# S5 outputs in one burst of matmuls over four groups of 32 output rows, S5 inputs as plain float32, two groups at a time

## The reference

```python
lam_bar = jnp.exp(lam * dt)
b_bar = ((lam_bar - 1.0) / lam)[..., None] * b_c
ug = u.astype(f32).reshape(bsz, seq, S5_GROUPS, S5_GROUP)
bu = jnp.einsum('blgh,gph->blgp', ug.astype(jnp.complex64), b_bar)
state = linear_scan(jnp.broadcast_to(lam_bar, bu.shape), bu)
y = jnp.einsum('blgp,ghp->blgh', state, c_c).real + d.astype(f32) * ug
y = jax.nn.gelu(y.reshape(bsz, seq, BRANCH))
y = y * jax.nn.sigmoid(y @ w_glu.astype(f32) + b_glu.astype(f32))
```

## Time and profile before

| | |
|---|---|
| runs shown | 2974.36 us median (2973.3 to 2975.58) |
| the profiled execution's own time | 2973.05 us |
| span of the profile | 2971.0 us |
| PE busy | 2894.8 us, 97% of the span |
| PE weight loads busy | 2454.7 us, 83% |
| DVE busy | 2010.5 us, 68% |
| ACT busy | 1582.0 us, 53% |
| POOL busy | 751.4 us, 25% |
| mean DMA rate | 176 GB/s |
| mean granted TensorE clock | 0.993 |

### The profile page before, as it was taken

One profiled execution on the slowest core, in us unless ns is written; L12 is line 12 of the kernel. 1 busy time (PEld: TensorE's weight loads), 2 busy tenths in 40 slices (PEclk: granted clock), 3 DMA queues, 4 the chain that ended last, 5 costly groups with the idle time before them and its releaser, 6 DMA issues.

```text
span 2971.0 us, 56245 instructions
## 1 busy us (share of the span) xinstructions
PE 2894.8 (97%) x16280; PEld 2454.7 (83%) x16280; DVE 2010.5 (68%) x3316; ACT 1582.0 (53%) x2828; POOL 751.4 (25%) x813
## 2 busy tenths in 40 slices
PE   6999999999999999999989999999999999999997
PEld 5878888888888888888877788888888888888886
DVE  7788888755555667555568888887555555665555
ACT  5555554565555655444455554546555655644443
POOL 3145445401000123111123544543000011221110
PEclk9999999999999999999999999999999999999998
DMA  6655555655555556777745555555555555577775
GB/s 225 213 174 159 162 159 154 170 170 168 159 158 164 165 156 195 209 214 209 206 142 174 167 162 159 159 162 171 171 157 164 160 168 154 158 213 209 215 209 176
DMA packets 276414, 522.69 MB, mean 176 GB/s; under 512 B 30912, under 2 KB 33872, under 8 KB 275280
## 3 DMA queue, kind: packets, MB, share of 16 engines
q1 hardware_dynamic: 257360, 477.13, 54.8%
q10 hardware_dynamic: 18944, 44.18, 4.5%
HBM read 508.60 MB, written 16.78 MB: 177 GB/s over the span
## 4 chain that ended last, share of the span: by engine, by line
PE 46%; DVE 2%; issue 2%; ACT 1%; DVEq 0%; POOL 0%; ACTq 0%; POOLq 0%
PE ps L294 26%; PE ps L293 13%; PE ps L443 1%; PE ps L337 1%; DVE w L975 1%; PE ps L456 0%; PE ps L452 0%; PE ps L296 0%; PE ps L325 0%; PE ps L338 0%; DVE zb L1523 0%; PE ps L326 0%; PE ps L327 0%; PE ps L304 0%; PE ps L313 0%
## 5 line engine op out<-in xcount | busy, mean ns | idle before, releaser
L294 PE MATMUL ps<-hb,w 128*128 128x512 f32 x5824 | 2059.1, 396 | 7.3 <-POOL hb L1553 6.1
L975 DVE TENSOR_TENSOR w<-raw,w 128x512 fp32r<-128x512 f32 x1760 | 1290.2, 738 | 859.5 <-ACT w L590 845.1
L590 ACT ACTIVATE w<-raw 128x512 fp32r<-128x512 f32 x1760 | 1098.2, 629 | 1138.6 <-PE ps L294 1135.9
L293 PE MATMUL ps<-hb,w 128*128 128x256 f32 x5690 | 1632.4, 287 | 13.2 <-DVE w L975 11.8
L294 PEld LDWEIGHTS ps<-hb,w 128*128 128x128 f32 x5824 | 1092.9, 188 | 250.5 <-issue 6.7
L293 PEld LDWEIGHTS ps<-hb,w 128*128 128x128 f32 x5690 | 1076.0, 189 | 70.8 <-issue 29.3
L294 PE MATMUL ps<-gl,w 128*128 128x512 f32 x640 | 226.6, 395 | 0.0
L1576 POOL TENSOR_TENSOR xx<-g,tab 128x512 f32<-128x512 f32 x64 | 121.0, 1891 | 269.6 <-DVE g L1038 269.1
L1703 POOL TENSOR_TENSOR nf<-zb 128x256 f32 (+1 forms) x60 | 51.9, 864 | 537.1 <-DVE zb L1491 531.6
L294 PE MATMUL ps<-w,hb 128*128 128x512 f32 x512 | 180.8, 395 | 0.0
L293 PE MATMUL ps<-gl,w 128*128 128x256 f32 x560 | 156.6, 280 | 0.0
(11 more groups left out here) (296 smaller groups left out, 2582.1 us busy)
## 6 DMA issues: line engine op xcount, KB each, us to landing
raw<-in_w SPq DMA_DIRECT2D x1763, 256.0 KB, 2.8
mlaw<-in_mlaw ACTq DMA_DIRECT2D x16, 768.0 KB, 4.2
mlaw<-in_mlaw ACTq DMA_DIRECT2D x16, 512.0 KB, 3.5
gate<-xres ACTq DMA_DIRECT2D x32, 256.0 KB, 4.5
xres<-zb ACTq DMA_DIRECT2D x32, 256.0 KB, 3.7
zb<-in_x SPq DMA_DIRECT2D x8, 512.0 KB, 7.5
xres<-in_x SPq DMA_DIRECT2D x4, 1024.0 KB, 7.0
s5w<-in_s5w ACTq DMA_DIRECT2D x16, 256.0 KB, 3.5
```

The costliest lines, as they stand in the source:

```text
L293: mm(acc[:, T:], a_lo, m_hi, start=False, stop=False, skip_group_check=True)
L294: last = mm(acc, a_hi, m_both, start=(k == 0), stop=(k == nk - 1), skip_group_check=True)
L590: A(w2[:, d, :, 0, :], raw[:, s, :, :], ACT.Copy).then_inc(hi_ready, 1)
L975: V.tensor_tensor(w2[:, d, :, 1, :], raw[:, s, :, :], w2[:, d, :, 0, :].bitcast(F), ALU.subtract).then_inc(w2_ready, 1)
```

## The change

Both kinds of S5 matmul are issued differently.

- **Inputs.** `us` is a plain float32 copy and B is read straight from `s5w`; the split is gone on ACT (one instruction of two) and DVE (both). `s5_in(it, q)` serves j = 2q and 2q+1 together: for each of real and imaginary part one float32 matmul on rows 64q to 64q+31 and one on the next 32 rows, into two different banks (`B_BU` and `B_B`). It is called twice an iteration, at step 29 of the pair before and at step 13.
- **Outputs.** The four states stay in four buffers (`xx`, and `kv`, `lg`, `gab`, which are the attention's and GLA's and idle in this stage), and `s5_out(it)` issues all eight matmuls at step 1 of the next pair, j running fastest. The four j have different 32 output rows and the same bank.
- `back` waits for PE only at j = 0; the fetch of the next B and C moves from ACT step 12 to 17.

```diff
@@ PE
-            def s5_in(it, j):
-                if j == 0:
-                    pe.wait_ge(us_split, it * 2 + 2)
-                pe.wait_ge(bu_read, it * 4 + (j + 1))
-                r = slice(32 * j, 32 * j + 32)
+            def s5_in(it, q):
+                if q == 0:
+                    pe.wait_ge(s5w_loaded, it * 16 + 16)
+                    pe.wait_ge(us_ready, it + 1)
+                pe.wait_ge(bu_read, it * 4 + (2 * q + 1))
                 for a in range(2):
-                    o = ps[:, B_BU, T * a:T * a + T]
-                    mm(o, bhi[r, a, :], us[r, 0, :], start=True, stop=False)
-                    mm(o, bhi[r, a, :], us[r, 1, :], start=False, stop=False)
-                    last = mm(o, blo[r, a, :], us[r, 0, :], start=False, stop=True)
+                    for j in (2 * q, 2 * q + 1):
+                        r = slice(32 * j, 32 * j + 32)
+                        last = mm(ps[:, BANKS_BU[j % 2], T * a:T * a + T], s5w[r, a, :], us[r, :],
+                                  start=True, stop=True)
                 last.then_inc(bu_ready, 1)
-            def s5_out(it, j):
-                if j == 0:
-                    pe.wait_ge(cprime_ready, it + 1)
-                    pe.wait_ge(s5_done, it + 1)
-                pe.wait_ge(state_ready, it * 4 + (j + 2))
-                o = ps[32 * j:32 * j + 32, B_Y, 0:T]
-                mm(o, cprime[:, 0, j, :], xx[:, 0, :], start=True, stop=False)
-                mm(o, cprime[:, 1, j, :], xx[:, 1, :], start=False, stop=True).then_inc(state_used, 1)
+            def s5_out(it):
+                pe.wait_ge(cprime_ready, it + 1)
+                pe.wait_ge(s5_done, it + 1)
+                pe.wait_ge(state_ready, it * 4 + 5)
+                for a in range(2):
+                    for j in range(4):
+                        last = mm(ps[32 * j:32 * j + 32, B_Y, 0:T], cprime[:, a, j, :], states[j][:, a, :],
+                                  start=(a == 0), stop=(a == 1), skip_group_check=True)
+                last.then_inc(state_used, 1)
             def s5_steps(it, first=False, more=True):
-                steps = {5: lambda: s5_in(it, 1), 9: lambda: s5_out(it, 0), 13: lambda: s5_in(it, 2),
-                         17: lambda: s5_out(it, 1), 21: lambda: s5_in(it, 3), 25: lambda: s5_out(it, 2)}
+                steps = {13: lambda: s5_in(it, 1)}
                 if not first:
-                    steps[1] = lambda: s5_out(it - 1, 3)
+                    steps[1] = lambda: s5_out(it - 1)
                 if more:
                     steps[29] = lambda: s5_in(it + 1, 0)
@@ ACT
-                act.wait_ge(bu_ready, it * 4 + 1)
-                A(us[:, 0, :], zb[:, g + Z_S5, :], ACT.Copy).then_inc(us_ready, 1)
-                act.wait_ge(s5w_loaded, it * 16 + 16)
-                A(bhi[:, :, :], s5w[:, 0:2, :], ACT.Copy).then_inc(us_ready, 1)
+                act.wait_ge(bu_ready, it * 2 + 1)
+                A(us[:, :], zb[:, g + Z_S5, :], ACT.Copy).then_inc(us_ready, 1)
@@ ACT s5_next
-                act.wait_ge(us_split, it * 2 + 2)
+                act.wait_ge(bu_ready, it * 2 + 3)
@@ DVE
-                steps[27] = steps[27] + [lambda: s5_split(it + 1, g + 1)]
@@ POOL back
-                pool.wait_ge(state_used, it * 4 + (j + 1))
-                G.tensor_tensor(xx[:, :, :], g2[:, :, :], tab[:, 0:1, :].to_broadcast([P, 2, T]),
+                if j == 0:
+                    pool.wait_ge(state_used, it + 1)
+                G.tensor_tensor(states[j][:, :, :], g2[:, :, :], tab[:, 0:1, :].to_broadcast([P, 2, T]),
```

More of the change, by code:

```diff
@@ L109, in trunk @@
         nf = sb("nf", [P, T])
-        us = sb("us", [P, 2, T], R)
-        bhi = sb("bhi", [P, 2, P], R)
-        blo = sb("blo", [P, 2, P], R)
+        us = sb("us", [P, T])
         yl = sb("yl", [P, T])
@@ L118, in trunk @@
         row = sb("row", [P, 8])
-        ga = sb("ga", [P, T])
-        gb = sb("gb", [P, T])
+        gab = sb("gab", [P, 2, T])
+        ga, gb = gab[:, 0, :], gab[:, 1, :]
         lg = sb("lg", [P, 2, T])
@@ L147, in trunk @@
         hf = (xx, yy, g2)
+        states = (xx, kv, lg, gab)
         kg = zb[:, Z_KG, :]
@@ L152, in trunk @@
         B_BU, B_Y, B_A, B_B = 4, 5, 6, 7
+        BANKS_BU = (B_BU, B_B)
         x_loaded = [sem(f"x_loaded{i}") for i in range(8)]
@@ L191, in trunk @@
             sem("silu_ready"), sem("glu_ready"), sem("glu_tanh"), sem("glu_squared"), sem("y2_ready"))
-        us_split, s5w_loaded, s5_done = sem("us_split"), sem("s5w_loaded"), sem("s5_done")
+        s5w_loaded, s5_done = sem("s5w_loaded"), sem("s5_done")
         s5_turned, s5_sin, lam_ready, lam_exp = sem("s5_turned"), sem("s5_sin"), sem("lam_ready"), sem("lam_exp")
@@ L405, in _ @@
                 steps = s5_steps(l * G8 + 7, more=False)
-                steps.update({3: k_turn, 6: k_sum, 33: lambda: s5_out(l * G8 + 7, 3), 46: latent_columns,
+                steps.update({3: k_turn, 6: k_sum, 33: lambda: s5_out(l * G8 + 7), 46: latent_columns,
                               50: lambda: spread([ps[:, B_B, 0:T], ps[:, B_B, T:]], c_l + 2), 70: glu_columns,
@@ L659, in s5_steps @@
             def s5_steps(it, g, more=True):
-                steps = {7: [lambda: s5_tables(it, 1)], 12: [lambda: s5_next(it)], 15: [lambda: s5_tables(it, 2)],
+                steps = {7: [lambda: s5_tables(it, 1)], 17: [lambda: s5_next(it)], 15: [lambda: s5_tables(it, 2)],
                          23: [lambda: s5_tables(it, 3)]}
@@ L1016, in y_mul @@
                                 ALU.mult).then_inc(hf_ready, 1)
-            bu = ps[:, B_BU, :].rearrange("p (a t) -> p a t", a=2)
+            bu = [ps[:, b, :].rearrange("p (a t) -> p a t", a=2) for b in BANKS_BU]
             def s5_rotate(it, j):
-                dve.wait_ge(bu_ready, it * 4 + (j + 2))
+                dve.wait_ge(bu_ready, it * 2 + (j // 2 + 2))
                 dve.wait_ge(tab_ready, it * 4 + (j + 2))
                 dve.wait_ge(state_ready, it * 4 + (j + 1))
-                own.do(V.tensor_tensor(yy[:, :, :], bu, tab[:, 0:1, :].to_broadcast([P, 2, T]), ALU.mult))
+                own.do(V.tensor_tensor(yy[:, :, :], bu[j % 2], tab[:, 0:1, :].to_broadcast([P, 2, T]), ALU.mult))
             def s5_rotate2(it, j):
-                V.tensor_tensor(g2[:, :, :], bu[:, ::-1, :], tab[:, 2:0:-1, :], ALU.mult).then_inc(bu_read, 1)
+                V.tensor_tensor(g2[:, :, :], bu[j % 2][:, ::-1, :], tab[:, 2:0:-1, :], ALU.mult).then_inc(bu_read, 1)
             def s5_sum(it, j):
@@ L1048, in s5_state @@
                 dve.wait_ge(back_ready, it * 4 + (j + 2))
[L1049 to L1057, removed]
+                V.tensor_tensor(states[j][:, :, :], states[j][:, :, :], yy[:, :, :], ALU.add).then_inc(state_ready, 1)
             def s5_tail(it, g):
-                dve.wait_ge(state_used, it * 4 + 5)
+                dve.wait_ge(state_used, it + 2)
                 own.wait()
@@ L1078, in s5_steps @@
                 steps[3] = ([] if first else [lambda: s5_tail(it - 1, g - 1)]) + [lambda: s5_scalars(g)] + steps[3]
-                if more:
-                    steps[27] = steps[27] + [lambda: s5_split(it + 1, g + 1)]
                 return steps
@@ L1274, in _ @@
                              13: [lambda: square_up(5, 1, 5)], 14: [lambda: square_up(5, 1, 5)], 16: [s5_turns],
-                             18: [s5_scale], 20: [s5_scale2], 22: [lru_softplus],
-                             27: [lambda: s5_split(l * G8, 0)]})
+                             18: [s5_scale], 20: [s5_scale2], 22: [lru_softplus]})
                 own.restart()
@@ L1586, in s5_cprime @@
                 pool.wait_ge(s5w_loaded, it * 16 + 16)
-                pool.wait_ge(state_used, it * 4 + 1)
+                pool.wait_ge(state_used, it + 1)
                 cr = s5w[:, 2, :].rearrange("p (j h) -> p j h", j=4)
```

## The result

The changed kernel takes 2887.57 us (median of four runs, 2884.39 to 2888.36) against 2974.97 us (2973.3 to 2976.61): a ratio of 0.9704, 95% interval 0.9687 to 0.9721. The profiled execution took 2887.51 us, 85.5 us less than the profiled one of before.

What follows compares the result with a forecast made beforehand. PE's matmul stream bounds the kernel, except where DVE is late in pair 2. Saved: 61.9 us in S5 calls, less 6.1 there, plus 1.3 of DVE relief, 57.1; 2915.9 profiled, 2917 us median, range 2893 to 2962.

Steps and rivals of the forecast that it cites:

- middle case: S5 calls: groups overlap but records start in program order; calls 1.44 and 2.25 us, 3.87 us saved an iteration; 54%.
- full overlap: S5 calls: all groups run side by side, calls 1.32 and 1.17 us, 78 us saved, 2896 us; chance 12%.
- the input's bound from single weight loads: S5 input calls, full overlap: 128-column weight loads no closer than 0.12 us, so eight records take 0.96 us, not 0.86.
- Pair 2's second half: Stretch once a layer where DVE is late: PE's saving of 3.06 us a layer, 6.1 us in all, doesn't count.
- The relief from the split: Pair 2's second half: DVE drops two split instructions of 0.67 us, saving 1.3 us for both layers.
- The clock: Pair 2's late-DVE stretch: more PE idling may lower the granted clock; only what lasts into pair 3 counts, 1 to 3 us.
- Entries and exits: PE's stream stopping around S5 calls: eight fall to three an iteration, 1.03 us in place of 2.68.
- the slower case: S5 calls: each of 13 group changes an iteration stops the stream some 0.2 us; +27 us, 3001 us; chance 9%.
- Edits at nothing: ACT's dropped copy of B, later B and C fetch, POOL's fewer waits, output burst's wait for last state: no time change.

Runs made afterwards that it cites:

- neighbours on the same group: Changed kernel with real and imaginary part innermost in both S5 calls, so matmuls on one group stand next to each other: 2886.94 us.
- short-form matmuls in twos: Changed kernel with inputs again in the short float form (split on ACT and DVE back), two row groups at a time: 2885.14 us, ratio 0.9708.
- The load on DVE there: Changed kernel with four more 128x512 operations on DVE in the second half of pair 2 of each layer: 2891.3 us.
- kernel with load in the steady pairs only: Changed kernel with four more 128x512 operations on DVE in each of the 14 other S5 iterations: 2891.18 us.
- the outputs alone: Output burst of the changed kernel with the inputs of the kernel before, split included: 2920.97 us, ratio 0.9826.
- the longer input call: Changed kernel with both j of an input call on the same 32 rows, leaving out the inputs of j = 1 and 3: 2914.84 us.

## Why the prediction was wrong

**The step that failed** is the middle case: "the two records of one float32 matmul need the same group. The second record of j = 0 must wait ... The first of j = 1 can start beside it", from "records start in the order of the program". The rows showed that order only within one group, where nothing else is possible, and I carried it over to several. The experiment with neighbours on the same group shows the order between groups doesn't bind: each group of rows or columns goes on as if served by itself. An output burst is 4 x 0.216 us and entry and exit, 1.20 us in place of 2.25; an input call 1.26 in place of 1.44. With the calls of before at 9.12 in place of 9.00, the calls gave 5.40 us an iteration in place of 3.87. In the 14 iterations outside pair 2 that is 21 us of the 28.4 by which the forecast for the profiled execution (2915.9) was high. The case "full overlap" had the mechanism and was given 12%; its calls, 1.32 and 1.17, were right to 0.06 us, the input's bound from single weight loads being too careful: short-form matmuls in twos show two loads of 128 columns side by side.

**The rest** of the error is mostly the pace of the chunks between the calls; the full case itself came to 2896 us. The steady pair fell by 54.04 - 48.21 = 5.83 us (from the end of chunk 0 to that of the next pair's chunk 0), the calls by 5.40. The other 0.43 us a pair are chunks that take 1.388 us each where they took 1.412 (the last section). I had taken the chunks as fixed. It would be 6 us in the 14 iterations; 4.5 are left, since the pair behind pair 2 in layer 1 gave only 4.3 us. The pairs 2 gave 1.5 us more than forecast, and the last 1 us lies outside the S5 pairs.

**Pair 2's second half** was placed rightly and sized too small. The pairs 2 gave 1.5 and 2.9 us in place of 5.83 each; so 7.3 us were lost where I had 6.1 less 1.3, or, for the full case, 6.4 less 1.3. The load on DVE there supports the mechanism. What I did not foresee is a stall of one S5 sub-step, which stands in both layers of the profiled run (last section). In the kernel with load in the steady pairs only it is absent, and there the pairs 2 took 43.61 us each, 3.0 and 4.1 less than before: by these the loss is 4.6 us, near the full case's 5.1. The relief from the split, 0.67 us a layer, can't be read apart.

**The clock**, which I named as a risk of 1 to 3 us, went the other way in the profiled executions. The kernel before had 3.4 us at half clock in the second half of pair 2 of each layer, the changed kernel had none in its S5 pairs, though PE waited longer. What that gave is not separated.

**Entries and exits** were read rightly: 0.32 to 0.40 us a call before and after, and three in place of eight are 1.7 us an iteration, a third of what was gained. No stop between groups exists, so the slower case falls: its 13 stops of 0.2 us an iteration would have been seen as starts 0.4 us apart.

**Edits at nothing** did cost nothing: the later fetch of B and C, POOL's waits and the output's wait for the last state held PE up nowhere, as the list of PE's waits shows no wait for a state or an input. DVE's busy time in a steady pair fell by 0.6 us (44.71 to 44.13), against 0.8 forecast.

## What to carry to other kernels

Small matmuls on different groups of 32 rows or 32 columns cost what the longest single group costs, in either order tried in the program: gather them, and count the records of one group only. This was seen for two groups of rows and for two and four groups of columns, with 256 columns streamed; rows and columns mixed were not tried. Short calls inside a dense stream of full matmuls pay about a third of a microsecond for entering and leaving, so two calls joined are worth that even without overlap. A chain of producers that ends in one buffer must be spread over several before its readers can be gathered; and where another engine holds a stretch, take that stretch out of the sum.

## What the runs showed of the hardware

**Groups pass each other.** The rounds of the reordered burst, above: the first record of `gab` at 1603.80, the second of `xx`, ahead of it in the program, at 1604.00. The Trainium skill, "TensorE: Matmul & The Clock Gate", section "Part 3: Packing small matmuls — row/col tiling", has matmuls start and end strictly in program order. For the starts the measurement differs, and decides; whether the ends keep the order was not tested. The Trainium skill's 4 ns between tiles, in the same section, is 7 ns here with one weight load and matmul for each, 13 ns with two.

**Two paces of the same stream.** Chunks of the same eight matmuls run at 1.388 or at 1.412 us, and a stretch keeps its pace until a readout or an S5 call breaks the stream. In the output projection of the changed kernel, where nothing but chunks is issued, the halves of a pair alternate, in the kernel before as well, with the slow half first there. PE's timeline in two halves, 13 and 12 pairs of matmuls apart:

```profile
1105.76 0.28 PE L293 MATMUL ps<-gl,w 128*128 128x256 f32 x1
...
1110.27 0.27 PE L293 MATMUL ps<-hb,w 128*128 128x256 f32 x1
...
1128.65 0.28 PE L293 MATMUL ps<-gl,w 128*128 128x256 f32 x1
...
1132.90 0.28 PE L293 MATMUL ps<-hb,w 128*128 128x256 f32 x1
```

4.51 / 13 = 0.347 us a pair of matmuls in the first, 4.25 / 12 = 0.354 in the second. From the first matmul start of a chunk of eight to the last are 1.156 us at the quick pace and 1.17 to 1.18 at the slow one. So counted, the kernel before had 573 quick and 688 slow chunks, the changed kernel 830 and 498: 190 fewer slow ones at 0.024 us are 4.6 us. A kernel's total can so move by some microseconds through nothing it does more or less of. What sets the pace was not tried and stays open.

**POOL and DVE stand in each other's way.** POOL's product of a sub-step (`back`) takes 1.65 us where it is quick. In the changed kernel's pair 2, layer 1, DVE went on at its usual pace, its rotation in 0.68 us, and POOL's product took 3.47 us. Where POOL's product takes 1.65 us it is DVE that is held: in layer 0 of the kernel with load in pair 2 the same rotation took 1.76 us. The timeline of POOL, then of DVE, then the wait of PE, in the changed kernel:

```profile
1585.37 3.47 POOL L1564 TENSOR_TENSOR lg<-g,tab 128x512 f32<-128x512 f32 x1 [3.07 <-DVE g L1036]
```

```profile
1585.79 0.68 DVE L1042 TENSOR_TENSOR yy<-g,tab 128x512 f32<-128x512 f32 x1
1586.39 1.28 DVE L973 TENSOR_TENSOR w<-raw,w 128x512 fp32r<-128x512 f32 x2
1588.94 0.69 DVE L1047 TENSOR_TENSOR lg<-lg,yy 128x512 f32<-128x512 f32 x1 [1.26 <-POOL lg L1564]
1591.07 1.29 DVE L973 TENSOR_TENSOR w<-raw,w 128x512 fp32r<-128x512 f32 x2 [1.44 <-ACT w L590]
```

```profile
1591.81 0.39 PE L293 MATMUL ps<-hb,w 128*128 128x256 f32 x1 [3.02 <-DVE w L973]
```

The state and ACT's tables wait for the product, the weights of the next chunks wait behind the tables on ACT, and PE waited 3.02 us for them, its longest wait for weights in the kernel. The same stands in layer 0. In the kernel with load in the steady pairs only, the same product took 1.65 us at this place and the half 20.5 us in place of 21.8. So the second half of pair 2 is held by this chain as much as by the sum of DVE's work. What decides which of the two engines is served first was not tried.

**After such a wait the clock can fall.** With the outputs alone, PE had a wait of 3.0 us of the same kind in pair 2 of each layer. Some 1.2 us after it went on, the granted clock fell to half, the lower of its two levels, and stayed there for 10.2 us. PE's timeline, and the window of the low clock (columns as above), in layer 1:

```profile
1613.09 0.39 PE L295 MATMUL ps<-hb,w 128*128 128x256 f32 x1 [3.01 <-DVE w L977]
```

```profile
1614.40:1624.60 10.20, 9.17 (x30) 7.06 (x29) 9.95 (x16) 4.80 (x11) 4.02 (x5) 0.50 0.60 180
```

These halves took 25.3 us, the longest of all, and the execution was 6 us or more slower than the other three of the same kernel (2927.69 us against 2919.61 to 2921.36), whose mean clock was 0.994 where it had 0.991. In the changed kernel the clock stayed full after the same wait; why is open. The halves of the ten profiles sort by these two things. Five with the quick product and full clock took 20.5 us, three with the slow product and full clock 21.8, two with the slow product and 6.8 us at half clock 23.7. The other ten carry the split, the load or the longer input call, and 3.4 us or more at half clock.
